# Each 128x128 turn in a mixture-of-experts kernel given as two turns of 64 rows

## The reference, cut to what matters

```python
def moe_ffn(h, router_w, router_b, w_gu, b_gu, w_down, b_down):
    ...
    logits = _f32(xf @ router_w + router_b)
    top_v, top_i = lax.top_k(logits, TOP_K)          # 4 of 32 experts for each of 512 tokens
    gates = jax.nn.softmax(top_v, axis=-1)
    ...
    xb = xf[row_tok].reshape(nb, EXPERT_BLOCK, D)     # blocks of 128 rows, one expert each

    def expert_block(args):
        x_blk, e = args
        gu = x_blk @ w_gu[e] + b_gu[e]                # 128x1024 by 1024x2048
        gate = jnp.minimum(gu[:, :D_FF], SWIGLU_LIMIT)
        up = jnp.clip(gu[:, D_FF:], -SWIGLU_LIMIT, SWIGLU_LIMIT)
        act = (up + 1.0) * (gate * jax.nn.sigmoid(SWIGLU_ALPHA * gate))
        return act @ w_down[e] + b_down[e]            # 128x1024 by 1024x1024
    ...
```

## Time and profile before

| what | value |
|---|---|
| runs | 1561.18, 1566.59, 1565.99 us |
| median | 1565.99 us |
| span of the profiled execution | 1562.1 us |
| TensorE busy | 1506.6 us (96%) |
| VectorE busy | 1380.6 us (88%) |
| ScalarE busy | 1006.1 us (64%) |
| moved by DMA | 507.16 MB, mean 325 GB/s |
| mean granted TensorE clock | 0.987 |

### The profile page before, as it was taken

One profiled execution on the slowest core, in us unless ns is written; L12 is line 12 of the kernel. 1 busy time (PEld: TensorE's weight loads), 2 busy tenths in 40 slices (PEclk: granted clock), 3 DMA queues, 4 the chain that ended last, 5 costly groups with the idle time before them and its releaser, 6 DMA issues.

```text
span 1562.1 us, 22575 instructions
## 1 busy us (share of the span) xinstructions
PE 1506.6 (96%) x8449; PEld 1179.3 (75%) x8449; DVE 1380.6 (88%) x1074; ACT 1006.1 (64%) x820; POOL 225.0 (14%) x236
## 2 busy tenths in 40 slices
PE   4999999998899999999999999999999999999996
PEld 2674468756688888888888888888888888888873
DVE  6888577487999999999999999999999999999997
ACT  4332433344577777777777777777777777777772
POOL 3343031000011111111111111111111111110061
PEclk9999999997999999999999999999999999999998
DMA  9788020216799999999999999999999999999992
GB/s 362 266 303 333 25 96 30 73 68 239 261 378 404 382 388 386 380 384 400 384 387 389 390 387 388 381 384 383 398 393 394 382 383 393 380 379 395 375 377 110
DMA packets 89144, 507.16 MB, mean 325 GB/s; under 512 B 11248, under 2 KB 12576, under 8 KB 37760
## 3 DMA queue, kind: packets, MB, share of 16 engines
q1 hardware_dynamic: 74256, 454.11, 74.3%
q0 software_dynamic: 9104, 34.08, 6.2%
q10 hardware_dynamic: 5728, 18.18, 2.9%
HBM read 477.51 MB, written 28.84 MB: 324 GB/s over the span
## 4 chain that ended last, share of the span: by engine, by line
PE 91%; DVE 5%; DMA 1%; ACT 1%; issue 1%; POOL 0%; SPq 0%; DVEq 0%; POOLq 0%; ACTq 0%
PE ps L2326 67%; PE ps L2342 2%; PE ps L1366 2%; PE ps L2305 2%; PE ps L1438 2%; PE ps L1352 2%; PE ps L1358 2%; PE ps L1355 2%; PE ps L1265 1%; DMA Wt<-in_ada_w 1%; PE ps L1360 1%; PE ps L2383 1%; PE ps L2315 1%; PE ps L2232 1%; PE ps L2249 1%
## 5 line engine op out<-in xcount | busy, mean ns | idle before, releaser
L1622 DVE TENSOR_TENSOR w_lo<-w_raw,w_hi 128x2048 fp32r<-128x2048 f32 x384 | 865.3, 2289 | 63.0 <-ACT w_hi L1616 59.2
L1616 ACT ACTIVATE w_hi<-w_raw 128x2048 fp32r<-128x2048 f32 x384 | 736.3, 1919 | 273.4 <-PE ps L2326 273.4
L2326 PE MATMUL ps<-w_hi,xTh 128*128 128x512 f32 x1024 | 406.2, 397 | 4.1 <-DVE xTl L2062 2.2
L2326 PE MATMUL ps<-w_lo,xTh 128*128 128x512 f32 x1024 | 400.0, 391 | 0.0
L2326 PE MATMUL ps<-w_hi,xTl 128*128 128x512 f32 x1024 | 275.0, 391 | 0.0
L2326 PEld LDWEIGHTS ps<-w_hi,xTh 128*128 128x128 f32 x1024 | 192.9, 188 | 51.2 <-issue 7.5
L2326 PEld LDWEIGHTS ps<-w_hi,xTl 128*128 128x128 f32 x1024 | 192.9, 188 | 40.5
L2326 PEld LDWEIGHTS ps<-w_lo,xTh 128*128 128x128 f32 x1024 | 192.8, 188 | 38.0
L2326 PE MATMUL ps<-w_hi,aTh 128*128 128x512 f32 x512 | 202.6, 396 | 0.0
L2326 PE MATMUL ps<-w_lo,aTh 128*128 128x512 f32 x512 | 199.5, 390 | 0.0
L1664 POOL TENSOR_TENSOR carried<-iotaE 128x1 f32<-128x1 f32 x64 | 27.9, 436 | 992.6 <-PE ps L2305 870.1
(11 more groups left out here) (425 smaller groups left out, 1590.6 us busy)
## 6 DMA issues: line engine op xcount, KB each, us to landing
w_raw<-in_moe_w_gu SPq DMA_DIRECT2D x256, 1024.0 KB, 6.6
w_raw<-in_moe_w_down SPq DMA_DIRECT2D x128, 1024.0 KB, 7.4
y_rows<-R ACTq DMA_DIRECT2D x30, 512.0 KB, 7.6
Wt<-in_ada_w SPq DMA_DIRECT2D x10, 1024.0 KB, 4.8
y_rows<-Wt POOLq DMA_DIRECT2D x1, 8704.0 KB, 24.6
Wt<-in_ada_w SPq DMA_DIRECT2D x16, 512.0 KB, 11.7
Wt<-in_w_in SPq DMA_DIRECT2D x4, 2048.0 KB, 9.7
R<-in_ada_w SPq DMA_DIRECT2D x6, 1024.0 KB, 8.3
```

Source lines behind the costliest of these rows:

```text
L1616: nc.scalar.activation(w_hi[:, at[-1] % HI_SLOTS, :], w_raw[:, at[-1] % RAW_SLOTS, :], ACT.Copy).then_inc(hi_rdy, 1)
L1622: nc.vector.tensor_tensor(w_lo[:, s, :], w_raw[:, s, :], w_hi[:, at[-1] % HI_SLOTS, :].bitcast(F32), ALU.subtract).then_inc(lo_rdy, 1)
L2326: ins = mm(ps[:, bank0 + c, :], x[:, k, :], w[:, 512 * (banks * i + c):512 * (banks * i + c) + 512], start=(first and i == 0 and x is xh a ...
```

## The change

Every turn of 128x128 becomes two turns of 64 rows. The first (rows 0 to 63) goes into bank 4, the second (rows 64 to 127) into bank 5, so that a bank holds the eight tiles' 64 columns of one half. The readers follow: `turned_ps` and `of_rows` describe the same 1024 values in runs of 64 that alternate between the banks. Two waits move in a step: `act_rdy` and `at_lo` with `xg_in` are now waited for before the last product of the chunk ahead of the turn, and not between that chunk and the turn.

```diff
+        by_rows = [slice(HD * r, HD * r + HD) for r in range(2)]
+        turned_ps = ps[:, 4:6, :].rearrange("p r (k t) -> p k r t", k=KT)
+        def of_rows(buf):
+            return buf.rearrange("p k (r t) -> p k r t", r=2)
...
-                s_.activation(dst[:], ps[:, 4:6, :].rearrange("p b (k t) -> p (b k) t", k=4), ACT.Copy
-                              ).then_inc(ev_sem, 1)
+                s_.activation(of_rows(dst[:]), turned_ps, ACT.Copy).then_inc(ev_sem, 1)
...
-                v.tensor_tensor(lo_part[:], ps[:, 4:6, :].rearrange("p b (k t) -> p (b k) t", k=4),
-                                hi_part[:].bitcast(F32), ALU.subtract).then_inc(lo_sem, 1)
+                v.tensor_tensor(of_rows(lo_part[:]), turned_ps, of_rows(hi_part[:].bitcast(F32)),
+                                ALU.subtract).then_inc(lo_sem, 1)
...
-            def xt(n, s, cnt):
-                pe.wait_ge(xg_in[s], 16 * cnt)
+            def xt(s):
                 for k in range(KT):
-                    ins = nc.tensor.transpose(ps[:, 4 + k // 4, P * (k % 4):P * (k % 4) + P],
-                                              xg[s][:, P * k:P * k + P], ident[:])
+                    for r, rows in enumerate(by_rows):
+                        ins = nc.tensor.transpose(ps[:, 4 + r, HD * k:HD * k + HD],
+                                                  xg[s][rows, P * k:P * k + P], ident[rows, rows])
                 ins.then_inc(xt_mm, 1)
...
                             for w in parts:
+                                if turn_next is not None and i == len(tiles) - 1 and x is xl and c == banks - 1:
+                                    turn_next()
                                 ins = mm(ps[:, bank0 + c, :], x[:, k, :],
...
-            def at_turn(n):
-                pe.wait_ge(act_rdy, n + 1)
+            def at_turn():
                 for k in range(KT):
                     j, i = k // 2, k % 2
-                    ins = nc.tensor.transpose(ps[:, 4 + k // 4, P * (k % 4):P * (k % 4) + P],
-                                              act_b[:, 2 * P * j + i:2 * P * (j + 1):2], ident[:])
+                    for r, rows in enumerate(by_rows):
+                        ins = nc.tensor.transpose(ps[:, 4 + r, HD * k:HD * k + HD],
+                                                  act_b[rows, 2 * P * j + i:2 * P * (j + 1):2], ident[rows, rows])
                 ins.then_inc(at_mm, 1)
...
+                def next_rows():
+                    pe.wait_ge(at_lo, n)
+                    if nxt is not None:
+                        rows_landed(1 - s, nxt)
                 for c in range(4):
-                    gate_up(where(c), c)
-                at_turn(n - 1)
+                    gate_up(where(c), c, (lambda: act_made(n - 1)) if c == 3 else None)
+                at_turn()
                 for c in range(4, KT):
-                    gate_up(where(c), c)
-                pe.wait_ge(at_lo, n)
+                    gate_up(where(c), c, next_rows if c == KT - 1 else None)
                 if nxt is not None:
-                    xt(n + 1, 1 - s, nxt)
+                    xt(1 - s)
```

More of the change, by code:

```diff
@@ L1756, in _ @@
                     act.wait_ge(lg_mm, t)
-                s_.activation(h2T, ps[:, 4:6, :].rearrange("p b (k t) -> p (b k) t", k=4), ACT.Copy).then_inc(h2t_ev, 1)
+                s_.activation(of_rows(h2T), turned_ps, ACT.Copy).then_inc(h2t_ev, 1)
             def turned(n, mm_sem, dst, ev_sem):
                 act.wait_ge(mm_sem, n + 1)
-                s_.activation(dst[:], ps[:, 4:6, :].rearrange("p b (k t) -> p (b k) t", k=4), ACT.Copy
-                              ).then_inc(ev_sem, 1)
+                s_.activation(of_rows(dst[:]), turned_ps, ACT.Copy).then_inc(ev_sem, 1)
             def xt_evac(n, e):
@@ L1830, in _ @@
             act.wait_ge(tail_mm, 1)
-            s_.activation(tailT, ps[:, 4:6, :], ACT.Copy).then_inc(gmt_rdy, 1)
+            s_.activation(of_rows(tailT.rearrange("p i (t c) -> p (i t) c", t=TT)), turned_ps, ACT.Copy).then_inc(gmt_rdy, 1)
             sigmoid(E - 1, place(E - 1, KT - 1))
@@ L2241, in turn @@
                 for k in range(KT):
-                    ins = nc.tensor.transpose(ps[:, 4 + k // 4, P * (k % 4):P * (k % 4) + P],
-                                              h2[t % 2][:, P * k:P * k + P], ident[:])
+                    for r, rows in enumerate(by_rows):
+                        ins = nc.tensor.transpose(ps[:, 4 + r, HD * k:HD * k + HD],
+                                                  h2[t % 2][rows, P * k:P * k + P], ident[rows, rows])
                 ins.then_inc(h2t_mm, 1)
@@ L2316, in bias, with rows_landed, act_made, chunk @@
                            start=(x == halves[0]), stop=False)
-            def chunk(at, tiles, xh, xl, banks, bank0, first, last):
+            def rows_landed(s, cnt):
+                pe.wait_ge(xg_in[s], 16 * cnt)
+            def act_made(n):
+                pe.wait_ge(act_rdy, n + 1)
+            def chunk(at, tiles, xh, xl, banks, bank0, first, last, turn_next=None):
                 hs, ls = at[-1] % HI_SLOTS, at[-1] % RAW_SLOTS
@@ L2330, in chunk, with gate_up @@
                 ins.then_inc(w_used, 1)
-            def gate_up(at, c):
-                chunk(at, (c,), xTh, xTl, 4, 0, False, c == KT - 1)
+            def gate_up(at, c, turn_next=None):
+                chunk(at, (c,), xTh, xTl, 4, 0, False, c == KT - 1, turn_next)
             def down(at, c):
                 chunk(at, (2 * c, 2 * c + 1), aTh, aTl, 2, 6, c == 0, c == 3)
-            def at_turn(n):
-                pe.wait_ge(act_rdy, n + 1)
+            def at_turn():
                 for k in range(KT):
                     j, i = k // 2, k % 2
-                    ins = nc.tensor.transpose(ps[:, 4 + k // 4, P * (k % 4):P * (k % 4) + P],
-                                              act_b[:, 2 * P * j + i:2 * P * (j + 1):2], ident[:])
+                    for r, rows in enumerate(by_rows):
+                        ins = nc.tensor.transpose(ps[:, 4 + r, HD * k:HD * k + HD],
+                                                  act_b[rows, 2 * P * j + i:2 * P * (j + 1):2], ident[rows, rows])
                 ins.then_inc(at_mm, 1)
@@ L2377, in tail_turn @@
                     for t in range(TT):
-                        ins = nc.tensor.transpose(ps[:, 4 + i, P * t:P * t + P], tailG[:, TT * i + t, :], ident[:])
+                        for r, rows in enumerate(by_rows):
+                            ins = nc.tensor.transpose(ps[:, 4 + r, HD * (TT * i + t):HD * (TT * i + t) + HD],
+                                                      tailG[rows, TT * i + t, :], ident[rows, rows])
                 ins.then_inc(tail_mm, 1)
@@ L2385, in tail_add @@
                 return ins
-            xt(0, 0, 1)
+            rows_landed(0, 1)
+            xt(0)
             pe.wait_ge(bias_lo, 1)
@@ L2403, in _ @@
                     ins.then_inc(gmt_mm, 1)
-            xt(1, 1, 1)
+            rows_landed(1, 1)
+            xt(1)
             ov = overflow_count(pe)
@@ L2416, in _ @@
             pe.wait_ge(gmt_rdy, 2)
-            at_turn(E - 1)
+            act_made(E - 1)
+            at_turn()
             pe.wait_ge(y_last, 1)
@@ L2434, in _ @@
                     pe.wait_ge(at_lo, n)
-                    xt(n, 0, E // 2 + 1 + j)
+                    rows_landed(0, E // 2 + 1 + j)
+                    nc.tensor.transpose(ps[:, 4, 0:P], xg[0][:, 0:P], ident[:])
+                    xt(0)
                     pe.wait_ge(act_rdy, n)
@@ L2439, in _ @@
                     for c in range(KT):
-                        gate_up(extra(j, c), c)
-                    at_turn(n)
+                        gate_up(extra(j, c), c, (lambda: act_made(n)) if c == KT - 1 else None)
+                    at_turn()
                     pe.wait_ge(at_lo, n + 1)
```

## The result

The changed kernel takes 1573.3 us (four runs, 1572.35 to 1573.76) against 1565.66 us (four runs, 1561.18 to 1566.59; three of them are those of the table above). The ratio is 1.005, with an interval of 1.0038 to 1.0062: 7.6 us slower, by the interval 5.9 to 9.7. The profiled executions differ by 9.4 us (1562.1 to 1571.5). The forecast was +8.6 us, just beyond the 0.5% (up to 1573.8 us) that it counted as no change. The result falls just inside that line, on the side to which the prediction gave 0.36, against 0.47 for slower. The interval of the ratio still says that the kernel is slower.

The account below looks back on a forecast made before the run. TensorE's own list bounds the kernel, 35 us a step; activation turns +10.5, x turns -1.7 and the first block's -0.3 sum to +8.6 us, so 1565.99 + 8.6 = 1574.6 us, 8-in-10 range 1555 to 1588.

Parts of the forecast that it names:

- The x turn: Turn of x in each step, split into halves: 0.82 us against 0.87 whole, -0.05 us each, 33 x -0.05 = -1.7 us.
- rival C: At x's turn a pair is no quicker than a whole turn was: x +0.33, activation +0.34, +21 us, 1587; chance 0.17.
- streaming term: In the split x turn, eight pairs of 64-row transposes side by side at 0.059 us each: 0.47 us.
- the load on the way in: First 64-row load of a split x turn, which nothing hides: 0.06 us, after 0.09 us until it starts.
- The activation's turn: Split activation turn, strided loads set 0.12 us a pair: 1.30 us against 0.96, +0.34 each, 31 x 0.34 = +10.5 us.
- Rival A: At the activation's turn, loads pair as quickly as x's (0.059): 0.88 against 0.96 us, about -5 us, 1561; chance 0.15.
- The change of shape: TensorE going into half arrays and out again at a turn: 0.33 to 0.40 us a round trip, seen at attention and bias.
- Rival B: At turns shape changes are free, first half load beneath the last whole product: -12.4 us, about 1553; chance 0.17.
- What was put at nothing: Moved waits in a step and new PSUM reading patterns of VectorE's and ScalarE's copies: no cost, hidden behind other work.
- rival D: A copy outgrows its cover: x's remainder takes twice its 1.2 us, +14 us beside the forecast's 8.6, 1589; chance 0.06.
- cover: At a step's start, 0.75 us between VectorE's first chunk ending and TensorE's load for it, hiding a slower x remainder copy.
- What lies outside the steps: Three x turns (second block, tail, router's second) at -0.05 us each, first block's -0.3, last activation turn 0.1, router's others nothing.

Follow-up runs that it names:

- the added pair: One extra pair of 64-row transposes ahead of each whole x turn, in the kernel with only the moved waits; 1577.87 against 1565.34 us before, ratio 1.0076.
- the best version: Changed kernel with the activation in neighbouring columns and the bias's 32-row products right behind its turn; 1553.71 us against 1565.87 for the kernel before, ratio 0.9921.

## Why the prediction was right

**What bounds the kernel.** Right: the 9.4 us of the span are TensorE's list, and no engine waits for another where it didn't before. The granted clock is 1.00 in the stretch, as before.

**The x turn.** 0.82 us was forecast and 0.83 measured, -0.05 and -0.04 by the starts. The pairs run side by side, as the timeline of the weight loads shows, first for this turn, then for the activation's:

```profile
731.11 0.57 PEld L2311 LDWEIGHTS ps<-ident,xg 64*128 64x128 f32 x16 [0.35 <-issue]
```

```profile
754.38 1.03 PEld L2356 LDWEIGHTS ps<-ident,R 64*128 64x128 f32 x16 [0.35 <-issue]
```

Sixteen loads of x take 0.57 us, so eight pairs of 0.14 us each start (0.57 - 0.14)/7 = 0.06 us apart. In the single records of all 32 turns the products of consecutive pairs start 0.061 to 0.064 us apart from the second pair on, and both halves of a pair within 0.006. This is where rival C falls. The forecast had 0.059, so its streaming term, 0.47, is some 0.02 short; the load on the way in is about 0.01 shorter than its 0.06, and the two nearly cancel. The first 64-row load stands 0.08 us behind the last whole slot (731.03 to 731.11); the forecast had 0.09.

**The activation's turn.** 1.30 us forecast, 1.29 measured; +0.34 both. By the row above the pairs start (1.03 - 0.21)/7 = 0.12 us apart (0.117 to 0.124 in the single records, from the second on), for half the rows load no faster: 212 ns against 207 in the earlier trace rows at the stride, 138 against 140 without it. Rival A falls with these pairs. Its time was right for another kernel: without the stride the halves do pair as x's do, and the split measured 5.0 us faster than before, where A had put about 5. Of these 5.0 us 2.8 are the layout's, which A doesn't contain, so the agreement with A's sum is chance.

The Trainium skill says that a weight load's time goes by its columns and not by its rows ("TensorE: Matmul & The Clock Gate", in the part on LDWEIGHTS). The 138 and 140 ns agree on the rows; that columns alone count does not hold here, since the same 128 columns take 212 or 138 ns with the stride.

**The change of shape.** With eight pairs of 0.062 us taken out, 0.33 of the x turn's 0.83 us are left for the round trip (0.35 forecast); with seven of 0.12 and the last streaming taken out, 0.40 of the activation's 1.29 (0.41 forecast). The loads of both kinds of turn stand idle before the first half load, in spite of the moved waits, and the added pair pays 0.35 us with whole turns around it. Rival B wanted a first load beneath the last whole product and a round trip under 0.25 us; neither is there.

**What was put at nothing.** The copies are as they were, 1016 and 1214 ns after, 1018 and 1214 before (groups by line; the changed kernel's rows):

```profile
L1766 ACT ACTIVATE xTh<-ps 128x1024 fp32r<-128x1024 f32 x32 | 32.5, 1016 | 0.0
L2067 DVE TENSOR_TENSOR xTl<-ps,xTh 128x1024 fp32r<-128x1024 f32 x32 | 38.8, 1214 | 0.9 <-ACT xTh L1766 0.9
```

So rival D falls by its price, not by its cover. The moved waits cost nothing by the kernel that has them alone. The loop for further blocks of an expert, where the change also sets one whole transpose ahead of x's turn, doesn't run here: the group of x's loads in the changed kernel holds 512, which are the 32 turns of 16.

**The sum.** The step was forecast at +0.34 - 0.05 = +0.29 us and is +0.294. The 9.1 us that 31 such steps make lie inside the interval of the medians, 5.9 to 9.7. The spans differ by more than the medians because single executions scatter: a run's time is some 1.75 us longer than its own span (1573.23 against 1571.5 us for the profiled one of the changed kernel), and by that the profiled execution of before lies 1.8 us under its median and that of the changed kernel 0.1 under its own. So the step is forecast to a hundredth of a microsecond, while the agreement of the totals, 8.6 and 7.6, is no better than the scatter lets it be. What lies outside the steps (the second block, the tail, the router, the last turn) was forecast at -0.4 us in all, and the span leaves +0.3 for it; that is too little to be told apart.

## What to carry to other kernels

Before halving a short product to run two side by side, see what holds it: streaming is nearly halved (0.109 to 0.062 us here), a weight load is not, and a load that reads every second column holds a 128-column transpose by itself; lay the operand out first. Every change between array shapes cost 0.15 to 0.2 us of TensorE's list here that no neighbour hid, so a halved turn must save more than the 0.33 to 0.40 us of a round trip, or share its change of shape with other small products, as the bias and the turn do in the best version. An engine's list that nobody delays can be added up from starts: 31 times one step gave the result within 2 us.

## What the runs showed that was not expected

From 64 to 32 rows is a change of shape too: the gap of 0.64 us from the turn's first start to the next load is the same for a bias of 32 rows as for a whole product.

VectorE reads PSUM and SBUF at every second column at no price: 1224 ns for 1024 columns as before, in the kernel with the new layout.

With the moved waits alone the first 48 products behind the bias took 11.13 us (705.38 to 716.51) instead of 11.10 and the step 35.22 instead of 35.19 us (the kernel with the added pair shows 11.13 too), while its runs were no slower; the changed kernel has the same waits and shows 11.09. By the single records these 0.03 us lie in the first ten products behind the bias, which start 0.224 to 0.236 us apart where the kernel before has 0.226 to 0.229. Why is open, and 31 times as much, some 1 us, is more than the runs show (-2.3 to +0.5 us by the interval).
